# The front of a hybrid decoder step: products of ones ahead of the data, a first row block in two pieces, three reorderings

## What is computed

```python
def project(x, pos, attn_norm, w_in, ...):
    h = rms_norm(x, attn_norm)
    z = jnp.einsum('btd,de->bte', h, w_in)
    q_a, ckv, krope, u, qm, gate = jnp.split(z, SPLIT_POINTS, axis=-1)
    ...
    krope = apply_rope(krope, cos, sin)
    ckv = rms_norm(ckv, kv_a_norm)

def mem_kv(mem, mem_norm, w_mem_kv):
    kv = jnp.einsum('bmd,de->bme', rms_norm(mem, mem_norm), w_mem_kv)
```

## Time and profile before

| | us |
|---|---|
| median of three runs | 941.05 |
| profiled execution, its own time | 940.15 |
| its span | 938.1 |
| PE busy | 916.6 (98%) |
| PE's weight loads busy | 825.7 (88%) |
| DVE busy | 537.1 (57%) |
| ACT busy | 436.5 (47%) |
| POOL busy | 43.8 (5%) |

### The profile page before, as it was taken

One profiled execution on the slowest core, in us unless ns is written; L12 is line 12 of the kernel. 1 busy time (PEld: TensorE's weight loads), 2 busy tenths in 40 slices (PEclk: granted clock), 3 DMA queues, 4 the chain that ended last, 5 costly groups with the idle time before them and its releaser, 6 DMA issues. The chain is left out here.

```text
span 938.1 us, 15409 instructions
## 1 busy us (share of the span) xinstructions
PE 916.6 (98%) x5649; PEld 825.7 (88%) x5649; DVE 537.1 (57%) x959; ACT 436.5 (47%) x740; POOL 43.8 (5%) x42
## 2 busy tenths in 40 slices
PE   6999999999999999999999999999999999999996
PEld 6999999999989899999999998888877888888884
DVE  6566444532475587787887558766576514134553
ACT  6764331122214567666677435677664403133221
POOL 0030003322100000000000000000100000000000
PEclk9999999999999999999999999999999999999998
DMA  9974452233452777778877526241351662224023
GB/s 364 330 239 157 134 195 90 68 111 116 168 220 94 224 240 246 238 237 259 246 248 238 187 100 220 79 146 34 108 209 44 213 213 91 90 88 153 6 90 112
DMA packets 76042, 155.95 MB, mean 166 GB/s; under 512 B 9256, under 2 KB 43625, under 8 KB 73976
## 3 DMA queue, kind: packets, MB, share of 16 engines
q1 hardware_dynamic: 74080, 146.51, 47.1%
q10 hardware_dynamic: 1888, 8.46, 2.5%
HBM read 143.56 MB, written 11.50 MB: 165 GB/s over the span
## 5 line engine op out<-in xcount | busy, mean ns | idle before, releaser
L67 PE MATMUL z<-x_hi,w_hi 128*128 128x288 f32 x512 | 153.6, 300 | 0.0
L69 PE MATMUL z<-x_hi,w_lo 128*128 128x288 f32 x512 | 150.8, 294 | 0.0
L68 PE MATMUL z<-x_lo,w_hi 128*128 128x288 f32 x512 | 150.8, 294 | 0.0
L184 ACT ACTIVATE w_hi<-w_raw 128x1024 fp32r<-128x1024 f32 (+2 forms) x62 | 64.9, 1047 | 166.4 <-PE z L69 78.8
L191 DVE TENSOR_TENSOR w_lo<-w_raw,w_hi 128x1024 fp32r<-128x1024 f32 (+2 forms) x62 | 76.8, 1239 | 77.4 <-ACT w_hi L184 76.9
L67 PEld LDWEIGHTS z<-x_hi,w_hi 128*128 128x128 f32 x512 | 96.0, 188 | 3.5 <-issue 1.1
L68 PEld LDWEIGHTS z<-x_lo,w_hi 128*128 128x128 f32 x512 | 96.1, 188 | 1.3 <-issue 0.2
L69 PEld LDWEIGHTS z<-x_hi,w_lo 128*128 128x128 f32 x512 | 96.1, 188 | 0.0
L1900 DVE TENSOR_TENSOR o_lo<-o_raw,o_hi 128x1024 fp32r<-128x1024 f32 x28 | 33.9, 1223 | 73.0 <-ACT o_hi L1743 73.0
L69 PE MATMUL z_acc<-x_hi,w_lo 128*128 128x288 f32 x256 | 75.1, 293 | 0.0
L1743 ACT ACTIVATE o_hi<-o_raw 128x1024 fp32r<-128x1024 f32 x28 | 29.5, 1059 | 72.6 <-PE pa_s L2402 26.7
(11 more groups left out here) (517 smaller groups left out, 2359.7 us busy)
## 6 DMA issues: line engine op xcount, KB each, us to landing
w_raw<-in_w_feat SPq DMA_DIRECT2D x56, 512.0 KB, 4.4
k_raw<-in_cache SPq DMA_DIRECT2D x128, 192.0 KB, 3.1
v_raw<-in_cache SPq DMA_DIRECT2D x128, 128.0 KB, 2.6
o_raw<-in_w_out SPq DMA_DIRECT2D x32, 512.0 KB, 4.0
w_raw<-in_w_mem_kv SPq DMA_DIRECT2D x16, 512.0 KB, 3.5
gate_spill<-gate_tmp SPq DMA_DIRECT2D x16, 288.0 KB, 3.4
mix<-gate_spill SPq DMA_DIRECT2D x4, 1152.0 KB, 9.6
x_nat<-in_x ACTq DMA_DIRECT2D x4, 1024.0 KB, 8.8
```

The costliest lines, as they stand in the source:

```text
L67: pe.matmul(out, a[0], b[0], start=start, stop=False)
L68: pe.matmul(out, a[0], b[1], start=False, stop=False)
L69: return pe.matmul(out, a[1], b[0], start=False, stop=stop)
L184: act.activation(hi_slot(s, u)[:, lo:w], s.wraw[:, u % RAW, lo:w], ACT.Copy).then_inc(s.w_hi, 1)
```

## The change

On PE, twelve products of `ones` by `ones` (128x128, f32) come ahead of `latents(0)`. Their result, in the first columns of `z_acc`, is not used; `memory(0)` starts that bank anew. They wait only until POOL has written `ones`.

Row block 0 of x is split in two pieces, columns 0 to 255 and 256 to 575, on ACT and on DVE, with a semaphore for the first piece of each (`x0_hi`, `x0_lo`). PE starts after the first and waits for the second ahead of its third tile of 128 tokens.

On SP, the tables are issued behind the memory units 0 and 1 instead of ahead of them, and mem chunks 1 to 3 behind the loads of rounds 1, 3 and 5 instead of ahead of them.

On DVE, the sample latents are added ahead of the split of memory unit 1 instead of behind it; the copies of the four banks stay behind it.

```diff
+FIRST_X, WARM = 2 * P, 12
...
                 mem_chunk(0)
-                load_units(sp, a, s, 5, 6)
+                load_units(sp, a, s, 5, feat_unit(0))
                 for dst, src in ((psc[:], a["pool_scale_c"]),
...
                 sp.dma_start(s0[:, 0:GR * DB * STATE], a["state_t"]).then_inc(st_in, 16)
-                for i in range(MIXED):
+                load_units(sp, a, s, feat_unit(0), feat_unit(0) + 1)
+                for i in range(1, MIXED):
+                    load_units(sp, a, s, mem_unit(2 * i), feat_unit(i) + 1)
                     if i in (1, 3, 5):
                         mem_chunk((i + 1) // 2)
-                    load_units(sp, a, s, mem_unit(2 * i), feat_unit(i) + 1)
...
-                        act.activation(xhi[:, k, :], xraw[:, k, :], ACT.Identity, scale=gx[:, k:k + 1]).then_inc(x_hi, 1)
+                        if k == 0:
+                            act.activation(xhi[:, 0, 0:FIRST_X], xraw[:, 0, 0:FIRST_X], ACT.Identity, scale=gx[:, 0:1]).then_inc(x0_hi, 1)
+                            act.activation(xhi[:, 0, FIRST_X:T], xraw[:, 0, FIRST_X:T], ACT.Identity, scale=gx[:, 0:1]).then_inc(x_hi, 1)
+                        else:
+                            act.activation(xhi[:, k, :], xraw[:, k, :], ACT.Identity, scale=gx[:, k:k + 1]).then_inc(x_hi, 1)
...
-                    dve.wait_ge(x_hi, k + 1)
-                    dve.scalar_tensor_tensor(out=xlo[:, k, :], in0=xraw[:, k, :], scalar=gx[:, k:k + 1],
-                                             in1=f32(xhi[:, k, :]), op0=ALU.mult, op1=ALU.subtract).then_inc(x_lo, 1)
+                    parts = ((slice(0, FIRST_X), x0_hi, x0_lo), (slice(FIRST_X, T), x_hi, x_lo)) if k == 0 else ((slice(0, T), x_hi, x_lo),)
+                    for cols, hi_done, lo_done in parts:
+                        dve.wait_ge(hi_done, k + 1)
+                        dve.scalar_tensor_tensor(out=xlo[:, k, cols], in0=xraw[:, k, cols], scalar=gx[:, k:k + 1],
+                                                 in1=f32(xhi[:, k, cols]), op0=ALU.mult, op1=ALU.subtract).then_inc(lo_done, 1)
...
                     memory(2 * i)
-                    memory(2 * i + 1)
-                    if i == 0:
+                    if i:
+                        memory(2 * i + 1)
+                    else:
+                        memory_rows(1)
                         dve.wait_ge(prep, 2)
                         dve.wait_ge(s.w_used, KV_UNITS)
                         dve.wait_ge(kv_low, 1)
                         dve.tensor_tensor(s.kvn[0:NS, 4, :], kv_bank(4)[0:NS], th[0:NS, 0:KV], ALU.add).then_inc(kv_raw, 1)
+                        split_lo(dve, s, mem_unit(1), mem_unit(1) + 1)
                         for r in range(4):
                             dve.tensor_copy(s.kvn[:, r, :], kv_bank(r)).then_inc(kv_raw, 1)
...
-                        pe.wait_ge(x_lo, k + 1)
+                        if k:
+                            pe.wait_ge(x_lo, k + 1)
+                        else:
+                            pe.wait_ge(x0_lo, 1)
                         for i in range(4):
+                            if k == 0 and P * i == FIRST_X:
+                                pe.wait_ge(x_lo, 1)
                             product(pe, kv_bank(i), (xhi[:, k, P * i:P * i + P], xlo[:, k, P * i:P * i + P]), w[kk], k == 0, k == KD - 1)
...
+                pe.wait_ge(ident, 2)
+                for _ in range(WARM):
+                    pe.matmul(z[:, 0, 0, 0:P], s.ones[:], s.ones[:], start=True, stop=True)
                 for u in range(KV_UNITS):
                     latents(u)
```

More of the change, by code:

```diff
@@ L255, in front_stage @@
         tail, tail_sb, st_in = sem("p_tail"), sem("p_tail_sb"), sem("p_state_in")
+        x0_hi, x0_lo = sem("p_x0hi"), sem("p_x0lo")
         w0_in, w0_hi, w0_lo, xs_hi, xs_lo, kv_low = sem("p_w0in"), sem("p_w0hi"), sem("p_w0lo"), sem("p_xshi"), sem("p_xslo"), sem("p_kvlow")
@@ L519, in _, with memory_rows @@
                         dve.tensor_copy(xs[:, part, NS:2 * NS], f32(xlo[:, part, SEQ:T])).then_inc(xs_lo, 1)
-                def memory(k):
+                def memory_rows(k):
                     dve.wait_ge(m_hi, k + 1)
@@ L524, in memory @@
                                              in1=f32(mhi[:, k, :]), op0=ALU.mult, op1=ALU.subtract).then_inc(m_lo, 1)
+                def memory(k):
+                    memory_rows(k)
                     split_lo(dve, s, mem_unit(k), mem_unit(k) + 1)
```

## The result

| | before | after |
|---|---|---|
| median, us (22 executions each) | 940.85 | 942.91 |
| lowest and highest | 940.0 and 941.17 | 940.29 and 946.09 |
| after over before | | 1.0027, 95% interval 1.0021 to 1.0034 |
| profiled execution, its own time | 940.15 | 940.29 |

The change made the kernel 0.27% slower, against a forecast of 0.15% faster. The executions also spread over 5.8 us where those before spread over 1.2. The profiled execution is the fastest of the 22, so this profile shows the loss at its smallest.

A forecast was written before the change was run, and what follows sets the result against it. PE was taken as bound by its 7.3 us wait before the first product and the lower clock in k=0. The front gains 1.45 us, the other edits cost nothing: 941.05 - 1.45 = 939.6 us, range 939.2 to 940.6.

The forecast's parts named there:

- The front: PE's start: row block k=0 begins at 6.70 at the upper clock, k=1 at 9.05; gain 1.45 us.
- the bound: Products of ones at PE's start: 5.3 to 5.8 us if wholly at the lower clock, ending at 6.3 to 6.8.
- `x_lo` of k=1: DVE's input for PE's second row block, hanging on chunk 1: ends at 8.90, so PE waits 0.6 us.
- The edit of the sample latents: DVE's add ahead of the memory unit 1 split, near 40 us: costed at nothing, bounds 0 and 0.3 us.
- The mem chunks: SP's mem chunks behind the feature half loads: chunk 1 wanted 10.8 us after half 1's load is freed; cost nothing.
- the cost of the tables' new place: Seven tables ahead of feature half 0's load: latency about 4.5 us, cost nothing, 0 to 3.5 at the ends.
- rival 2: Feature half 0 lands 8.4 us after issue, as `state_t` did: stall 3.5 us, time 943.1; chance 0.04.
- Both bounds, 3.8 and 8.4: Latency of feature half 0's load: 3.8 us, its own before, to 8.4, that of `state_t` in a loaded queue.
- 4.9 us until PE waits: Feature half 0's load may come 4.9 us after its issue before PE has to wait.
- rival 1: Feature half 0 lands 5 to 7 us after issue behind the tables: at 5.8, stall 0.9, time 940.5; chance 0.13.

The follow-up runs named there:

- e4: Changed kernel with the whole of SP's issue order, tables and mem chunks, as in the kernel before: 939.39 us, ratio 0.999.
- e1: Changed kernel with the seven tables issued ahead of memory units 0 and 1 again, as in the kernel before: 939.51 us, ratio 0.9983.
- e5: Changed kernel with the seven tables issued behind feature half 0's load, ahead of memory unit 2: 939.27 us, ratio 0.9983.
- e10: Changed kernel with the seven tables issued behind feature half 1's load and mem chunk 1: 939.0 us, ratio 0.998.
- after_look_2: The changed kernel unaltered, one more profiled execution: 944.5 us.
- e8: Changed kernel with the two large tables ahead of memory units 0 and 1 again, the five small ones left behind: 939.57 us, ratio 0.9991.
- e2: Kernel before with only the seven tables moved behind memory unit 1: 942.12 us, ratio 1.0013.
- e6: Changed kernel with the tables early again and the sample latents added behind DVE's split of memory unit 1 again: 940.01 us, ratio 0.9992.
- e3: Kernel before with only the twelve products of ones added: 939.82 us, ratio 0.9992.
- e9: Changed kernel with mem chunk 1 also issued in front of feature half 0's load, behind the tables: 943.57 us, ratio 1.0034.
- after_look_3: The changed kernel unaltered, a further profiled execution: 944.89 us.
- e7: Changed kernel without the twelve products of ones: 941.76 us, ratio 1.001.
- after_again: The changed kernel unaltered, run once more for a second profile: 940.61 us.

## Why the prediction was wrong

**The front was right.** k=0 came at 6.57 (forecast 6.70) at the pace of 0.147, and the clock did not fall in the idle time before it, since there was none: the ones ran longer than I took as likely (to 6.56, at 5.3 to 5.8 us as the bound said), and this cost nothing. The gain was limited by `x_lo` of k=1, as worked out; the lead was 1.71 us instead of 1.45, since that block was ready at 8.71 instead of 9.05, by the chance told above. In the medians of the kernels without the tables in the way it is 1.0 to 1.7 us (e4, e1, e5, e10).

**The edit of the sample latents** at 0 cost nothing that shows, and its bound of 0.3 was too small on the side of a gain: about 0.7 us when memory unit 1's load is late, by four profiles. **The mem chunks** at 0: right (e4).

**The step that failed** is the cost of the tables' new place: "I take about 4.5, near its own", and with it the argument against rival 2 that the x rows "are down by then". Both bounds, 3.8 and 8.4, were in hand, and I chose the lower because it was the load's own row. But that row was taken with no table in front of the load; the change put seven transfers there. The row for a load behind those transfers was the other one. The reason given for the lower one, that mem chunk 1 now comes later, was worth nothing: e4 has the chunk in its old place, and the latency is 5.2 us against 5.1 in e1. The x rows were not down either: ACT issues the fifth row load (`x_nat`) at 35.6 us, and it took 7.0 us to land in the profile after. Measured latencies of the changed kernel are 6.3 to 10.1 in five profiles, so 8.4 was not an upper bound either. The wait they give is 1.2 to 4.6 us where the sum had 0. The rule "4.9 us until PE waits" was right to 0.2 in all but the longest.

**A term was missing**: the clock. I had it in mind for the start of the program only. In the three profiles with a wait of over 3 us at half 0 the lower clock costs 1.5 to 2.6 us more behind it.

**The rivals.** What happened is rivals 1 and 2, in turn: 1 in the short executions, 2 in the long ones. Rival 2 with its 943.1 us is close to the median, at a chance of 0.04, but by luck: it has no term for the clock, and an execution with nearly its latency (8.3 us, after_look_2) took 944.5. The range held neither, since it went only to the middle of rival 1. The medians of e1, e5, e8 and e10 agree with the rule of the Trainium skill named there ("DMA: Bandwidth & Descriptors", Queues, rings and completion order), that each DMA engine takes the descriptors of one queue in order; but they would agree with a mere sharing of the engines too, as the table says. The Trainium skill's remark that the number of slow products at the start differs ("TensorE: Matmul & The Clock Gate", the section on the HAM clock gate) had no consequence in the changed kernel, as the sum said. It agrees with e2, where the pace rose 4.9 us after the first product in place of 3.1.

## What to carry to other kernels

A load that must come in time is priced with the queue that it will have, not with the latency that it had: where a change puts transfers in front of it, the row to take is that of a transfer that had some in front of it. Transfers that nobody needs for 20 us belong behind the last tight load (here 0.4% of the time: 939.0 against 942.98 in one session), or ahead of the units before it (e1), and not directly ahead of it. When PE runs ahead of its former time, each fixed margin behind shrinks and the next one shows (half 0, then memory unit 1); and a wait in the middle of the products (here of 1.8 to 4.6 us) can cost more than its length, since the clock may fall.

## What the runs showed that I had not expected

After a stop of PE of 1.8 to 4.6 us the granted clock read 0.50 for 3 to 7 us in five profiles (e6, e3, after_look_2, e9, after_look_3), although PE was at work again. The price was 1.52 us at a wait of 4.59 and 2.58 at one of 3.16, so the longer wait was not the dearer one. Nor does the length alone say whether the clock falls: it did not after 2.52 us in e7 and after 1.72 to 1.81 in e5, after and after_again, but it did after 1.83 us in e6 (rows below). The rest of the two memory units then took 5.82 us in e6, from the second tile of memory unit 0 to half 0, against 4.24 in e1, so the price there was 1.6 us.

```profile
44.00:45.00 1.00, 1.00 (x5) 0.83 (x6) 1.00 (x3) 0.80 (x1) 0.00 (x0) 1.00 0.14 57
45.00:46.00 1.00, 1.00 (x5) 0.76 (x4) 1.00 (x3) 1.00 (x2) 0.00 (x0) 0.67 0.00 0
46.00:47.00 1.00, 1.00 (x4) 0.80 (x3) 0.62 (x1) 1.00 (x2) 0.00 (x0) 0.50 0.18 70
```

In e3, after a stop of 2.95 us, the products of 512 columns started 0.43 us apart from 45.16 to 48.15, in place of 0.23:

```profile
44.68 0.68 PE L67 MATMUL z_acc<-w_hi_more,mem_hi 128*128 128x512 f32 x1 [2.95 <-DVE kvn L547]
45.16 0.63 PE L68 MATMUL z_acc<-w_lo,mem_hi 128*128 128x512 f32 x1
...
48.15 0.45 PE L69 MATMUL z_acc<-w_hi,mem_lo 128*128 128x512 f32 x1
48.44 0.40 PE L67 MATMUL z_acc<-w_hi,mem_hi 128*128 128x512 f32 x1
```

And one load of one kernel had latencies from 6.3 to 10.1 us in five executions of the same program: a change that removes a margin shows first as a spread, and the one profile shown may be the best case.
